# Two token tiles under the arriving weights in the input projection, and the last output tile in two halves

## The reference

```
proj = rmsnorm(x, norm_in) @ w_in           # (tokens, 1024) @ (1024, 1696 + 1024 gate)
cq, ckv, kr, qb, kb, vb, qc, gate = split(proj)
cq, ckv normed; rope on kr, on a quarter of qb and kb
...                                          # attention branches A, B, C
y = rmsnorm(x + (concat(o_a, o_b, o_c) * silu(gate)) @ w_out, norm_final)
```

## Time and profile before

| | us |
|---|---|
| median of 3 runs | 2078.2 (2067.97 to 2080.51) |
| the profiled execution | 2075.85 |
| its span, first to last instruction | 2074.2 |
| PE busy in the span | 1934.3 (93%) |
| DVE busy | 1080.4 (52%) |
| ACT busy | 932.6 (45%) |
| POOL busy | 425.2 (20%) |
| mean granted TensorE clock | 0.972 of full |

### The profile page before, as it was taken

The page is one execution under the profiler, slowest core; times in us unless marked ns, Lnnn a source line. Parts: engine busy times, 40 slices in busy tenths (PEclk is TensorE's granted clock), DMA queues, the critical chain, the costliest instruction groups (busy, mean ns, idle before and its releaser), DMA issues. The chain is left out here.

```text
span 2074.2 us, 47175 instructions
## 1 busy us (share of the span) xinstructions
PE 1934.3 (93%) x17532; PEld 1468.7 (71%) x17532; DVE 1080.4 (52%) x3163; ACT 932.6 (45%) x2106; POOL 425.2 (20%) x584
## 2 busy tenths in 40 slices
PE   6999999788877989999999989999999989999997
PEld 5888888466655876667666656666666668888886
DVE  4334242476795447767776645555555753232332
ACT  4333332377863225556555634444444543333332
POOL 0111111233463313113311142222222200000000
PEclk9999999897999999999999999999999989999999
DMA  8333333442356552011201189877875452332331
GB/s 293 101 114 100 114 100 94 120 155 92 120 147 162 145 168 88 21 45 43 65 17 25 47 258 287 245 227 231 230 223 196 127 206 83 110 91 81 98 101 44
DMA packets 178426, 270.37 MB, mean 130 GB/s; under 512 B 28088, under 2 KB 138632, under 8 KB 169336
## 3 DMA queue, kind: packets, MB, share of 16 engines
q1 hardware_dynamic: 158456, 169.74, 28.8%
q0 software_dynamic: 19808, 98.40, 14.0%
HBM read 213.06 MB, written 54.76 MB: 129 GB/s over the span
## 5 line engine op out<-in xcount | busy, mean ns | idle before, releaser
L75 PE MATMUL proj_acc<-proj_w_hi,proj_x_hi 128*128 128x512 f32 (+2 forms) x544 | 197.7, 363 | 19.0 <-DVE proj_x_lo L299 12.4
L76 PE MATMUL proj_acc<-proj_w_lo,proj_x_hi 128*128 128x512 f32 (+2 forms) x544 | 196.1, 360 | 0.0
L77 PE MATMUL proj_acc<-proj_w_hi,proj_x_lo 128*128 128x512 f32 (+2 forms) x544 | 195.7, 360 | 0.0
L1660 ACT ACTIVATE mla_probs<-mla_probs,mla_bias 128x256 f32<-128x256 f32 (+15 forms) x128 | 153.0, 1196 | 11.6 <-DVE mla_bias L1724 7.3
L1720 DVE CUSTOM_DVE_ANT_0 mla_probs<-mla_scores,mla_zero 128x512 f32<-128x512 f32 x192 | 124.7, 687 | 59.1 <-PE mla_scores L1576 58.8
L75 PEld LDWEIGHTS proj_acc<-proj_w_hi,proj_x_hi 128*128 128x128 f32 x544 | 104.1, 191 | 32.3 <-DVE proj_x_lo L299 12.4
L818 ACT ACTIVATE win_probs<-win_probs,win_bias 128x256 f32<-128x256 f32 (+1 forms) x256 | 117.4, 462 | 17.9 <-DVE win_bias L857 17.6
L2045 PE MATMUL dec_scores<-dec_keysT,sample_q_lat 128*64 128x512 f32 x512 | 122.7, 600 | 2.2 <-DVE dec_krT L2211 1.2
L353 DVE COPY proj_featT<-proj_tr 128x512 f32<-128x512 f32 x34 | 23.5, 691 | 188.1 <-PE proj_tr L406 186.4
L2233 DVE COPY dec_pT<-dec_p_turned 128x256 f32<-128x256 f32 x80 | 33.9, 424 | 157.7 <-PE dec_outs L2061 129.7
L77 PEld LDWEIGHTS proj_acc<-proj_w_hi,proj_x_lo 128*128 128x128 f32 x544 | 103.8, 191 | 13.0
(11 more groups left out here) (407 smaller groups left out, 5003.9 us busy)
## 6 DMA issues: line engine op xcount, KB each, us to landing
win_v_tile<-wv_out SPq DMA_DIRECT2D x75, 128.0 KB
proj_x_raw<-in_xT SPq DMA_DIRECT2D x17, 512.0 KB, 6.2
proj_rows<-in_x SPq DMA_DIRECT2D x17, 512.0 KB, 5.3
featT<-proj_featT POOLq DMA_DIRECT2D x34, 256.0 KB, 2.8
late_ckv<-in_xT SPq DMA_DIRECT2D x17, 512.0 KB, 7.0
host_buf<-mix SPq DMA_DIRECT2D x17, 512.0 KB, 3.6
late_ckv<-in_x SPq DMA_DIRECT2D x17, 512.0 KB, 4.1
y_out<-host_buf POOLq DMA_DIRECT2D x17, 512.0 KB, 6.4
```

Source lines behind the costliest of these rows:

```text
L75: pe.matmul(out, lh, rh, start=start, stop=False)
L76: pe.matmul(out, lh, rl, start=False, stop=False)
L77: return pe.matmul(out, ll, rh, start=False, stop=stop)
L1660: act.activation(row, row, ACT.Exp, bias=bias[:, at:at + 1], scale=-1.0, accum_out=total[:, at:at + 1]).then_inc(exp_done, 1)
```

## The change

In the input projection:

- The ring of weight buffers has five places instead of three; `memT` and `mem_rows` serve as the two more until the memory data is loaded.
- Slice 0 is loaded in two pieces, its first 416 columns ahead of everything; token tile 0 comes next, and token tile 1 after slice 1. A small copy on ACT runs right after the gains arrive.
- While the weights come, PE works on tile 0 and, two slices behind, on chunks 0 and 1 of tile 1, which go into `mem_acc`. Chunks 2 and 3 of tile 1 follow once tile 0's have been read out of `acc`.
- Rotary table, rows and constants of tile 0 move behind slices 6 and 7. Token tiles are loaded one tile earlier, rotary tables have a semaphore of their own.
- Transposes of tiles 1 to 15 use three PSUM banks, the third being `mem_acc[:, 1]`; tiles 0 and 16 keep two.

In the output projection, for the last tile alone: the sum of squares and the final scaling are done in halves of 512 columns, and SP stores the halves instead of POOL. An ACT root without a user follows the first half's squares.

```diff
+        w_from = [w_raw[:, r, :] for r in range(RAW)] + [t[:].rearrange("p a b -> p (a b)")[:, 0:W_COLS] for t in (memT, mem_rows)]
+        RING = len(w_from)
+        HEAD = CHUNKS[0][1]
+        three = [tr[:, 0, :, :], tr[:, 1, :, :], mem_acc[:, 1, :].rearrange("p (j t) -> p j t", t=P)]
+        two = three[0:2] + three[0:1]
...
+            sp.dma_start(w_from[0][:, 0:HEAD], io["w_in"][0:P, 0:HEAD]).then_inc(head_loaded, 16)
+            load_early(0, x_first)
             load_weights(0)
...
+            load_weights(1)
+            load_early(1, x_second)
+            for k in range(2, DK):
                 load_weights(k)
+                if k == DK - 2:
+                    load_rest(0)
+                if k == DK - 1:
+                    sp.dma_start(kv_gain[:], io["kv_gain"].rearrange("(o n) -> o n", o=1).broadcast_to([P, KVL])).then_inc(consts, 16)
+                    sp.dma_start(q_gain[:], io["q_gain"].rearrange("(o n) -> o n", o=1).broadcast_to([P, QL])).then_inc(consts, 16)
+                    sp.dma_start(ident[:], io["ident"]).then_inc(consts, 16)
...
             sp.sem_inc(staging_free, 2)
-            load(1, 0, 1)
+            load_x(2, 0)
+            load_rest(1)
...
                 for u in range(2):
-                    load(i * 2 + u, i, u)
+                    load(i * 2 + u, u)
+                    load_x(i * 2 + u + 1, 1 - u)
                     store(i * 2 + u - 2, u)
...
+            tile(0, 0, 0, acc, ahead=2)
+            tile(1, 0, 1, mem_acc, ahead=0)
+            with act.Fori(1, NT_PROMPT // 2) as i:
...
-            by_chunk = 3
+            by_chunk, behind = 1, 2
             for k in range(DK - by_chunk):
                 for c in range(NC):
-                    first(c, k)
+                    if c == (0 if k else 1):
+                        pe.wait_ge(w_low, k + 1)
+                    first(0, c, k)
+                if k >= behind:
+                    if k == behind:
+                        pe.wait_ge(x_low, 4)
+                    for c in range(MT):
+                        first(1, c, k - behind)
...
+            for c in range(MT):
+                for k in range(DK - by_chunk - behind, DK):
+                    mm = first(1, c, k)
+                mm.then_inc(proj_done, 1)
+            project(1, 1, 2)
+            project(1, 1, 3)
+            transposes(0, 0, into=two, free=(1, 2, 3))
+            tile(2, 0, after_early=True)
+            with pe.Fori(1, NT_PROMPT // 2) as i:
...
+            for c, cols in enumerate(HALVES):
+                sp.wait_ge(normed, LAST + 3 + c)
+                sp.dma_start(io["y_out"][LAST * P:NT * P, cols], out[:, cols]).then_inc(last_stored, 16)
+            sp.wait_ge(last_stored, 32)
...
-            with pool.Fori(0, NT) as n:
+            with pool.Fori(0, LAST) as n:
...
+                if back and not split:
+                    for c, cols in enumerate(HALVES):
+                        act.wait_ge(summed, n * 2 + 1 + c)
+                        act.activation(junk[:, cols], rows[:, 1 - u, cols], ACT.Square, accum_out=last_ss[:, c:c + 1]).then_inc(squared, 1)
+                        if c == 0:
+                            act.activation(table[:], v[:, u:u + 1], ACT.Sqrt)
...
+                    for cols in HALVES if not split else [slice(0, D)]:
+                        dve.scalar_tensor_tensor(out[:, cols], rows[:, w, cols], r[:, w:w + 1], f_gain[:, cols], ALU.mult, ALU.mult).then_inc(normed, 1)
```

More of the change, by code:

```diff
@@ L248, in tile @@
                 act.activation(sq[:, u, 2:3], v[:, u, 2:3], ACT.Sqrt).then_inc(sq_done, 1)
-                if not last:
+                if ahead == 1:
                     split(n + 1, k if u == 0 else k + 1, 1 - u)
+                elif ahead == 2:
+                    split(n + 2, k + 1, u)
                 act.wait_ge(r_done, n + 1)
@@ L263, in tile, with split_weights, split_early @@
                 act.activation(qc[:, u, :], acc[:, 3, 0:256], ACT.Copy, scale=r[:, u, 0:1]).then_inc(act_evac, 1)
+            def split_weights(k, cols, loaded, count, high):
+                act.wait_ge(loaded, count)
+                act.activation(w_hi[:, k, cols], w_from[k % RING][:, cols], ACT.Copy, scale=gain[:, k:k + 1]).then_inc(high, 1)
+            def split_early(u, early):
+                act.wait_ge(early, 16)
+                act.activation(x_hi[:, u, :, :], x_raw[:, u, :, :], ACT.Copy).then_inc(x_high, 1)
             act.wait_ge(gained, 16)
+            act.activation(junk[:, 0:DK], gain[:], ACT.Copy)
+            split_weights(0, slice(0, HEAD), head_loaded, 16, head_high)
+            split_early(0, x_first)
             for k in range(DK):
[L267 to L271, removed]
+                split_weights(k, slice(0 if k else HEAD, W_COLS), w_loaded[k % RING], 16 * (k // RING + 1), w_high)
+                if k == 1:
+                    split_early(1, x_second)
             act.wait_ge(consts, 48)
-            act.wait_ge(x_loaded[0], 32)
-            with act.Fori(0, NT_PROMPT // 2) as i:
+            tile(0, 0, 0, acc, ahead=2)
+            tile(1, 0, 1, mem_acc, ahead=0)
+            with act.Fori(1, NT_PROMPT // 2) as i:
                 for u in range(2):
-                    tile(i * 2 + u, i, u)
-            tile(NT_PROMPT, NT_PROMPT // 2, 0, last=True)
+                    tile(i * 2 + u, i, u, acc)
+            tile(NT_PROMPT, NT_PROMPT // 2, 0, acc, ahead=0)
             act.wait_ge(mem_loaded, 64)
@@ L299, in split, with tile @@
                 dve.tensor_tensor(x_lo[:, u, :, :], x_raw[:, u, :, :], x_hi[:, u, :, :].bitcast(F32), ALU.subtract).then_inc(x_low, 1)
-            def tile(n, u, last=False):
+            def tile(n, k, u, acc_of, ahead=1, into=three):
                 links = [0]
@@ L315, in tile @@
                 dve.tensor_scalar(v[:, u, 1:3], v[:, u, 1:3], EPS, None, ALU.add).then_inc(v_done, 1)
-                if not last:
+                if ahead == 1:
                     split(n + 1, 1 - u)
+                elif ahead == 2:
+                    split(n + 2, u)
                 dve.wait_ge(sq_done, n + 1)
@@ L367, in _ @@
                 dve.tensor_scalar(mem_w[:, k, :], mem_w[:, k, :], mem_gain[:, k:k + 1], None, ALU.mult).then_inc(mem_gained, 1)
-            tile(NT_PROMPT, 0, last=True)
+            tile(NT_PROMPT, NT_PROMPT // 2, 0, acc, ahead=0, into=two)
             dve.wait_ge(mem_squared, MT)
@@ L392, in project, with transposes @@
                 mm.then_inc(proj_done, 1)
-            def transposes(n, u):
+            def transposes(n, u, into=three, free=None):
                 pe.wait_ge(rope_done, n + 3)
@@ L443, in _ @@
                 mm.then_inc(mem_projected, 1)
-            transposes(NT_PROMPT, 0)
+            transposes(NT_PROMPT, 0, into=two, free=(0, 1, 3))
             pe.wait_ge(mem_kept, MT)
```

130 lines of the change are left out of this document (72 added, 58 removed).

## The result

| | before | after |
|---|---|---|
| median of 20 runs each | 2078.9 us (2068.0 to 2084.1) | 2062.7 us (2056.1 to 2074.9) |
| ratio of the times | | 0.9924, 95% interval 0.991 to 0.9938 |
| profiled execution | 2075.85 | 2063.13 |
| its span | 2074.2 | 2061.5 |
| PE busy in the span | 1934.3 (93%) | 1928.1 (94%) |

The change makes the kernel 15.8 us faster (2078.9 x 0.0076; 12.9 to 18.7). The forecast was a gain of 18.1 and a time of 2058, in a range of 2048 to 2068. The gain is under 1%, the prediction's bound for what one measurement can tell; 20 runs of each kernel tell it.

The account below looks back on a forecast made before the run. PE, busy 93% of the span, was taken to bound the kernel, so gains come from its gaps, slow spells, start and end. 9.4 + 7.2 + 1.5 = 18.1 us, giving 2058 us, range 2048 to 2068 (forecast case alone 2052 to 2063).

Parts of the forecast that it names:

- PE's start near 8.6: Input projection start: PE's first matmul near 8.6 us instead of 12.4, a gain not kept because slices bind next.
- Arrival of slices: Weight loads at the start: slice 2 arrives at 13.5, PE has it at 17.3, later slices arrive 2.2 us apart.
- Part 1: Start of the input projection: tile 2 starts at 55.5 instead of 64.97, gain 9.4 us, ends 6.9 and 10.8.
- Each further step 3.62, no more waits for weights: Input projection from slice 2: each slice brings 3.62 us of PE work, more than the 2.2 us between arrivals.
- The new wait, 2.3, released by `vb`: Before chunk 2 of tile 1: PE waits 2.3 us for tile 0's `vb` out of `acc`, ending at 43.8.
- The clock loss of 1.4 behind it: Chunks 2 and 3 of tile 1: slow matmuls after PE's 2.3 us wait lose 1.4 us, as after the earlier idle.
- the clock holds: Rival, after PE's 2.3 us wait: no clock loss, delivery a little faster; gain 20 to 22, 2054 to 2056; chance 0.15.
- Part 2: Transposes of tiles 1 to 15, third bank: 0.48 us saved per tile, 7.2 us in all, ends 5.3 and 7.7.
- Part 3: End of the output projection, last tile's halves and SP's store: gain 1.5 us, ends 0.5 and 2.2.
- the rival that the moved work starts cold: Input projection start: idles or late slices leave PE at 1.2 GHz into step 3; 2061 to 2063 us; chance 0.17.
- The slower rival: After the wait at 41.5, PE keeps 1.2 GHz; over 36 us of it would eat 18 us; chance 0.02.

Follow-up runs that it names:

- c_warm: Changed kernel with slice 0 whole and first, tile 2 split after tile 0's readout; added: token tile 1 behind slice 2, 28 unused early PE matmuls. 2052.4 us, ratio 0.9867.
- the late split: Changed kernel, but ACT and DVE split token tile 2 only after tile 0's readout; median 2057.1 us, ratio to the kernel before 0.9894.
- the one-piece run: Changed kernel, but the last tile's row scaled and stored by SP in one piece; 4.8 us from last scaling to end of span.

## Why the prediction was right, point by point

The forecast held in sign and within 2.3 us of the measured gain. The time came out 4.7 above 2058, mostly because the forecast started from 2075.6, while 20 runs of the kernel before have a median of 2078.9. Of its steps:

- **PE's start near 8.6**: 8.30. Right. That this is not kept, because slices bind next, was right as well, and more so than I wrote: starting before the rest of slice 0 is there brought nothing that a trace shows.
- **Arrival of slices**: the term of Part 1 that was mis-sized. Slice 2 was to be at ACT at 13.5, and was at 15.6 (14.6 in the second profile); PE had it at 19.4 (18.4), not 17.3. Two things are in this. Token tile 1 ahead of it was priced at 1.3, from the rate between slices 2 and 3 of the kernel before (0.39 MB/us). But slice 2 reaches ACT 3.8 behind slice 1, where slices with nothing between them are 2.1 apart, so the tile costs 1.7. It does so with slice 0 whole too, and in `c_warm` between slices 2 and 3. The rest is slice 1 itself: it reaches ACT at 10.7 to 11.9 in the five profiles with the changed kernel's loads, and at 10.1 to 10.2 in the three variants that load slice 0 whole. With the whole slice more bytes move from 1.5 to 8.5 us (2.00 to 2.07 MB against 1.76 to 1.93). Why, and whether the cut or the order does it, was not tried.
- **Each further step 3.62, no more waits for weights**: 18.08 for five. Right.
- **The new wait, 2.3, released by `vb`**: 2.31. Right, and the late split shows its cause.
- **The clock loss of 1.4 behind it**: the spell was there in the profile (clock 0.64 over 4.6 us; chunks 2 and 3 took 1.6 longer than 8.5 and transposes allow). It was absent in the second profile of the same kernel after a wait of the same length. So on this point the forecast and the rival "the clock holds" are each true in some executions; of the seven profiles with the wait of 2.3, five have the spell.
- **Part 1**: 7.0 in the first profile, 9.6 in the second, forecast 9.4 with ends 6.9 and 10.8. Both are counted from 64.97; in the other two profiles of the kernel before tile 2 starts at 64.15 and 64.25, and the gain is 0.7 to 0.8 less.
- **Part 2**: 0.56 per tile instead of 0.48, 8.4 instead of 7.2, above the upper end of 7.7. The distance from one tile's transposes to the next tile's is 19.87, forecast 19.96. I had counted twelve transposes at their distance of 0.109; when no group waits the next product follows at 1.23, closer than 12 x 0.109 = 1.31.
- **Part 3**: 3.1 instead of 1.5, above the upper end of 2.2. Squares and scaling in halves gave 0.1, not 0.4. SP's first data left 0.7 after the scaling in the one-piece run, against 1.7 for POOL before: 1.0 instead of 0.35. The halves gave 0.5, not 0.75; the prediction had read eight slices of data in the earlier trace rows, where there are seven, 1.4 us. And 1.5 was in no term of the sum: the time from the last data to the end of the span, 4.1 with POOL and 2.6 with SP. It is half of the 3.1. The Trainium skill, page "DMA: Bandwidth & Descriptors", section "Latency and other measured facts", would have given an estimated 0.4 for the queue by its first-byte figures. Measured are 2.2 to 2.4 for the whole store, of which 0.7 to 0.9 lies before the last data.

Parts 2 and 3 were under by 2.8 together, Part 1 over by 2.4 in the profile: the sum was right partly because these cancel, which is luck. The measured 2062.7 lies at the upper edge of the forecast's own 2052 to 2063, and inside the 2061 to 2063 of the rival that the moved work starts cold, so the time alone can't part the two. By the trace that rival was half there: PE's first matmuls run slow (0.63 for 512 columns from 13.25 to 15.4 us), but in slice 1, from 16.87 on, they took 0.40 again. The slower rival did not occur; no slow spell up to tile 2 was longer than about 4 us. Slice 2 came 2.1 later than forecast. The Trainium skill's limit of about 358 GB/s from HBM ("DMA: Bandwidth & Descriptors", "Where 436 GB/s comes from") would put it an estimated 0.2 to 0.9 later. The trace does not agree with that limit: behind slice 2 the next slices of 868 KB reached ACT 2.1 us apart (15.59, 17.70, 19.80), which is 0.41 MB/us.

## What to carry to other kernels

When an engine starts earlier, look at the second piece of data, not the first: three matmuls at 8.3 us and then nothing until 12.7 gave no more than one start at 11 us with everything there. A short wait on PE costs its length and, in five of seven profiles, two thirds as much again behind it. Moving two splits that PE did not need yet behind the readout took 2.1 us of wait away, and no spell followed: a reordering alone. Where two things bind at the same time, as the slow first matmuls and slice 2 did, expect little from either cure alone. And price a closing store from the end of the last computation to the end of the span: who issues it mattered three to four times as much as halving it.

## What the hardware showed unexpectedly

- The same wait of 2.3 us on PE is sometimes followed by about 3 us at half pace and sometimes not, with identical code (57.94 and 55.39 for the start of tile 2).
- PE's first work (8.30 to 9.5 and 12.66 to 16.5 in the kernel after) runs slow, 0.55 and 0.63 for 416 and 512 columns instead of 0.35 and 0.40, though the granted clock of such a stretch reads 1.00. These are the lengths that go with a reading of 0.50 elsewhere: 0.55 for 416 columns from 44.20 in the kernel before, 0.63 for 512 from 47.7 in the kernel after. In the run in which PE had been busy before, the first matmuls aren't slow.
- The granted clock of the untouched window stage varied between 0.87 and 0.98 over the 14 profiles, and its length between 251 and 236 us, longest at the lowest clock. That is more than either part of this change. The stages behind it vary as well, from 1029.9 to 1044.2 us.
- From the last data of the closing store to the end of the span pass 4.1 us when POOL issues it and 2.6 when SP does.
